# The PEER layer in one block: choosing the gathered tiles' experts during the scores, with three early fetch slots in unwritten rows

## What is computed

```python
def _peer(x, w_q, sub_keys, u_table, v_table):       # x: 512 tokens of 1024
    q = (xb @ w_q).reshape(t, PEER_HEADS, 2, PEER_HALF)          # 8 heads, 2 sides, 128
    s = jnp.einsum('thpd,hpkd->thpk', q, sub_keys)               # 128 keys a side
    top_s, top_i = lax.top_k(s, K)                               # K = 16
    cand_s = top_s[:, :, 0, :, None] + top_s[:, :, 1, None, :]
    cand_i = top_i[:, :, 0, :, None] * PEER_N_KEYS + top_i[:, :, 1, None, :]
    best_s, best_pos = lax.top_k(cand_s.reshape(t, PEER_HEADS, K * K), K)
    idx = jnp.take_along_axis(cand_i..., best_pos, axis=-1)      # 16 of 16384 experts a head
    gate = jax.nn.softmax(best_s, axis=-1)
    h = jax.nn.gelu(jnp.einsum('thkd,td->thk', u_table[idx], xb))
    return jnp.einsum('thk,thkd->td', gate * h, v_table[idx])
...
x = _layer_norm(DN_ALPHA * x + _peer(x, ...), ln2_g, ln2_b)
```

## Time and profile before

| | |
|---|---|
| median of 3 runs | 2939.73 us (2935.13 to 2944.8) |
| profiled execution, time | 2941.49 us |
| its span, first to last instruction | 2938.8 us |
| mean granted TensorE clock | 0.917 |
| busy: PE, DVE, ACT, POOL | 85%, 66%, 36%, 23% of the span |
| DMA moved | 646.82 MB, mean 220 GB/s |
| block peer starts | about 1784 us |
| hidden rows end, products end | about 2303, 2746 us |
| last dot, last add | about 2489, 2927 us |

### The profile page before, as it was taken

One profiled execution on the slowest core, in us unless ns is written; L12 is line 12 of the kernel. 1 busy time (PEld: TensorE's weight loads), 2 busy tenths in 40 slices (PEclk: granted clock), 3 DMA queues, 4 the chain that ended last, 5 costly groups with the idle time before them and its releaser, 6 DMA issues. The chain is left out here.

```text
span 2938.8 us, 32174 instructions
## 1 busy us (share of the span) xinstructions
PE 2486.3 (85%) x11638; PEld 1856.6 (63%) x11638; DVE 1944.8 (66%) x3302; ACT 1058.6 (36%) x1868; POOL 668.4 (23%) x626
## 2 busy tenths in 40 slices
PE   4988759999969998768889898999999999999300
PEld 2875547888856865567777687889988644444100
DVE  5648448888853245755536478976878555666998
ACT  3248437788843246411013331117776000000000
POOL 0000012112210000200000001334544444644674
PEclk7999859999989999889889999999999999999755
DMA  7850255887742312200012224778999999999997
GB/s 272 261 200 31 58 229 219 318 310 271 296 175 62 95 53 56 81 22 1 1 40 91 76 74 175 262 277 298 362 345 338 367 383 396 410 409 409 410 408 263
DMA packets 254877, 646.82 MB, mean 220 GB/s; under 512 B 25216, under 2 KB 123776, under 8 KB 239232
## 3 DMA queue, kind: packets, MB, share of 16 engines
q1 hardware_dynamic: 172640, 367.89, 34.9%
q0 software_dynamic: 82080, 276.88, 24.9%
HBM read 654.11 MB, written 34.60 MB: 234 GB/s over the span
## 5 line engine op out<-in xcount | busy, mean ns | idle before, releaser
L2664 POOL DMA_INDIRECT sp_rows<-in_u_rows,sp_flat x256 | 292.6, 1143 | 992.8 <-DVE sp_flat L3010 615.3
L2673 DVE SCALAR_TENSOR_TENSOR sp_rows<-sp_rows,sp_x 128x1024 f32<-128x1024 f32 x256 | 313.8, 1227 | 160.9 <-DMA sp_rows<-in_u_rows,sp_flat 158.6
L284 DVE TENSOR_TENSOR wide_low<-wide_raw,wide_high 128x2048 fp32r<-128x2048 f32 x138 | 312.5, 2291 | 63.3 <-ACT wide_high L277 61.2
L170 DVE TENSOR_TENSOR w_low<-raw,w_high 128x1024 fp32r<-128x1024 f32 x106 | 129.7, 1225 | 279.0 <-ACT w_high L161 278.4
L2788 PE MATMUL ps<-xT,raw 128*128 128x256 f32 x1248 | 279.7, 381 | 12.5 <-PEq L2420 12.5
L277 ACT CAST wide_high<-wide_raw 128x2048 fp32r<-128x2048 f32 x138 | 261.5, 1914 | 21.9 <-PE ps L334 15.8
L2816 PE MATMUL ps<-raw,tb_made 128*128 128x512 f32 x608 | 265.3, 592 | 0.0
L2788 PEld LDWEIGHTS ps<-xT,raw 128*128 128x128 f32 x1248 | 235.5, 191 | 43.4 <-issue 12.7
L2816 PEld LDWEIGHTS ps<-raw,tb_made 128*128 128x128 f32 x608 | 115.4, 190 | 144.9 <-issue 144.9
L2682 DVE SCALAR_TENSOR_TENSOR sp_x<-sp_rows,sp_coef,sp_x 128x1024 f32<-128x1024 f32 x128 | 162.9, 1286 | 48.7 <-DMA sp_rows<-in_v,sp_flat 43.2
L2682 DVE SCALAR_TENSOR_TENSOR sp_x<-xT,sp_coef,sp_x 128x1024 f32<-128x1024 f32 x128 | 163.6, 1286 | 45.9 <-DMA xT<-in_v,sp_flat 45.4
(11 more groups left out here) (515 smaller groups left out, 5244.7 us busy)
## 6 DMA issues: line engine op xcount, KB each, us to landing
wide_raw<-in_w_experts SPq DMA_DIRECT2D x96, 1024.0 KB
raw<-in_u SPq DMA_DIRECT2D x78, 512.0 KB
raw<-in_v SPq DMA_DIRECT2D x76, 512.0 KB
tb_ring<-in_v SPq DMA_DIRECT2D x52, 512.0 KB
tb_ring<-in_u SPq DMA_DIRECT2D x50, 512.0 KB
ada_raw<-in_ada_w SPq DMA_DIRECT2D x24, 1024.0 KB, 7.3
raw<-in_w_in SPq DMA_DIRECT2D x42, 512.0 KB, 3.8
raw<-in_attn_w_in SPq DMA_DIRECT2D x24, 512.0 KB, 4.5
```

The costliest lines, as they stand in the source:

```text
L170: self.m.nc.vector.tensor_tensor(self.m.w_low[:, n % AHEAD, :], self.m.raw[:, n % RAW, :], self.m.w_high[:, n % AHEAD, :].bitcast(F32), AL ...
L284: self.m.nc.vector.tensor_tensor(self.low_of[:, n % self.READY, :], self.raw[:, n % self.RAW, :], self.high_of[:, n % self.READY, :].bitca ...
L2664: self.m.nc.gpsimd.indirect_dma_start(out=self.ring[self.slot(g)], out_offset=None, in_=src, in_offset=bass.IndirectOffsetOnAxis(ap=self.f ...
L2673: self.m.nc.vector.scalar_tensor_tensor(out=rows, in0=rows, scalar=1.0, in1=self.x[:, tile, :], op0=ALU.mult, op1=ALU.mult, accum_out=self ...
```

## The change

peer_scores is gone; its work is the first part of peer's block, with no barrier between.

- DVE searches only tiles 2 and 3 in the scores. After chunk 9's low part (LOWS_FIRST = 10) and the searches of heads 0 to 3 it chooses tile 2's heads 0 to 3. The low parts of the later chunks are made in that choice's steps (low_step, ten of them).
- Then it searches heads 4 to 7, chooses the other half of tile 2, and tile 3; then searches (in groups of four) and chooses tile 0 and tile 1.
- choose works on a range of heads. EARLY_DOTS holds 66 dots, ROW_DOTS two or three a row. The softmax of tiles 2 and 3 comes after the last dot.
- The first 64 fetches use three slots in activation rows 48 to 59 (FIRST_AT), so ACT's row 48 waits for 64 dots. Fetch 64 waits for the other half of tile 2 and for the last weight chunk, and uses the old slots.
- FIRST_QUAD is 60 (was 56). Eight transposes of x (tile 2) come between two chunks of the queries, the other eight after the scores.

The core of the diff:

```diff
-EARLY = (2, 3, 0)
-ORDER_TILES = (2, 3, 0, 1)
-FIRST_QUAD = 56
+FIRST_QUAD = 60
+FIRST_DOTS, FIRST_AT = 64, 48
...
+        self.first = [words[:, FIRST_AT * DT + k * D:FIRST_AT * DT + (k + 1) * D] for k in range(3)]
...
     def slot(self, g):
-        return g % GATHERS if g < DOTS else (g - DOTS) % LATE_GATHERS
+        if g < FIRST_DOTS:
+            return g % len(self.first)
+        return (g - FIRST_DOTS) % GATHERS if g < DOTS else (g - DOTS) % LATE_GATHERS
...
+        if g in (0, FIRST_DOTS, SLOTS_EACH):
+            pool.wait_ge(self.flat_made, (0, FIRST_DOTS, SLOTS_EACH).index(g) + 1)
+        if g == FIRST_DOTS:
+            self.m.stream.done(pool, "peer_q", 2 * HEADS - 1)
+        if g == DOTS + GATHERS:
             pool.wait_ge(self.spare_free, 1)
...
-    early = [0] * 10 + [1] * 10 + [1] * 10 + [2] * 5 + [1] * 10
-    rows = [2 if r > FIRST_QUAD else 0 for r in range(KEYS)]
+    tops, choice = [1, 2, 2, 2], [1] * 10
+    early = tops + [1, 0] * 5 + choice + 2 * ([3] * 4 + choice)
+    rows = [2 + r % 2 if r > FIRST_QUAD else 0 for r in range(KEYS)]
...
+            for n in range(2, HH + 1):                     # PE
+                if n < HH:
+                    queries(n)
+                score(n - 1)
+                if n == X_TURNS[0] - 1:
+                    pe.wait_ge(shifted, KT)
+                    turn_x(0)
+            turn_x(1)
             for r in range(KEYS):
                 hidden(r)
...
             def row(r):                                    # ACT
                 act.wait_ge(table.used, r + 1)
+                if r == FIRST_AT:
+                    act.wait_ge(sparse.consumed, FIRST_DOTS)
...
+            def low_of(n):                                 # DVE
+                if n < HH:
+                    m.stream.done(dve, "peer_q", n)
+                    m.stream.low(dve, "peer_q", n)
+            def top_keys(h):
+                dve.wait_ge(copied, 2 * h + 2)
+                first_tops(nc, link, table, [(tt, 2 * h + side) for tt in SPARSE for side in range(2)])
...
-            for n in range(TT):
-                choose(n)
-                finish(n)
-                if n >= 1:
+            for n in range(LOWS_FIRST):
+                low_of(n)
+                if n % 2 == 1 and n >= 3:
+                    top_keys((n - 3) // 2)
+            choose(SPARSE[0], 0, HEADS // 2, low_step)
+            for h in range(HEADS // 2, HEADS):
+                top_keys(h)
+                step()
+            choose(SPARSE[0], HEADS // 2, HEADS, step)
+            choose(SPARSE[1], 0, HEADS, step)
+            for n, tt in enumerate(DENSE):
+                for a in range(0, 2 * HEADS, 4):
+                    first_tops(nc, link, table, [(tt, k) for k in range(a, a + 4)])
+                    step()
+                if n:
                     softmax(n - 1)
-            softmax(TT - 1)
+                choose(tt, 0, HEADS, step)
+            softmax(len(DENSE) - 1)
...
             dots(DOTS)
+            for n in range(len(DENSE), TT):
+                softmax(n)
...
-EXP_ROWS = (6, 16, 28, 46)
+EXP_ROWS = (36, 54, 125, 126)
+DIFFED_AT = (4, 5, 2, 3)
+LOWS_FIRST = 10
```

More of the change, by code:

```diff
@@ L2641, in slot, with rows @@
     def slot(self, g):
-        return g % GATHERS if g < DOTS else (g - DOTS) % LATE_GATHERS
+        if g < FIRST_DOTS:
+            return g % len(self.first)
+        return (g - FIRST_DOTS) % GATHERS if g < DOTS else (g - DOTS) % LATE_GATHERS
+    def rows(self, g):
+        k = self.slot(g)
+        if g < FIRST_DOTS:
+            return self.first[k]
+        return (self.ring + self.late)[k]
     def which(self, g):
@@ L2681, in add @@
             dve.wait_ge(self.consumed, g - len(SPARSE) + 1)
-        self.m.nc.vector.scalar_tensor_tensor(out=self.x[:, tile, :], in0=self.ring[self.slot(g)],
+        self.m.nc.vector.scalar_tensor_tensor(out=self.x[:, tile, :], in0=self.rows(g),
                                               scalar=self.coef[:, tile, s:s + 1], in1=self.x[:, tile, :],
@@ L2763, in _ @@
         def _(sp):
-            for k in range(RAW, 2 * KEYS):
+            sp.dma_start(keys, m.i["keys"].rearrange("p (h k) -> p h k", k=KEYS)).then_inc(keys_loaded, 16)
+            for n in range(HH):
+                m.stream.load_after(sp, "peer_q", n)
+            sp.wait_ge(m.split_done, m.stream.total)
+            for k in range(2 * KEYS):
+                if k == RAW:
+                    m.stream.done(sp, "peer_q", HH - 1)
                 table.load(sp, k)
@@ L2933, in step, with rest @@
                 dots(next(early))
-            def every(n, one):
-                for k in range(n - 1):
-                    one(k)
-                link(one(n - 1))
-            def choose(n):
-                tt = ORDER_TILES[n]
-                val, idx, idxf, cand, crest, best, pos = (table.val[:, tt], table.idx[:, tt], table.idxf, table.cand, table.crest,
-                                                          table.best, table.pos)
-                part, whole, parts, ranks, eq = table.part, table.whole, table.parts, table.ranks, table.eq
-                e4 = crest.rearrange("p h c -> p (h c)").rearrange("p (a h k) -> p a h k", a=len(STRIPS), k=K)
-                if tt not in EARLY:
-                    for h in range(0, 2 * HEADS, HEADS):
-                        first_tops(nc, link, table, [(tt, a) for a in range(h, h + HEADS)])
-                    for _ in range(5):
-                        step()
+            def rest(k):
+                dve.wait_ge(highs, k + 1)
+                nc.vector.scalar_tensor_tensor(out=low[:, k, :], in0=m.xT[:, k, :], scalar=m.v("ln1_b")[:, k:k + 1],
+                                               in1=high[:, k, :].bitcast(F32), op0=ALU.add, op1=ALU.subtract
+                                               ).then_inc(lows, 1)
@@ new lines, in _, with low_step, choose, every @@
+            later_lows = iter(range(LOWS_FIRST, HH))
+            def low_of(n):
+                if n < HH:
+                    m.stream.done(dve, "peer_q", n)
+                    m.stream.low(dve, "peer_q", n)
+            def low_step():
+                low_of(next(later_lows, HH))
+            def top_keys(h):
+                dve.wait_ge(copied, 2 * h + 2)
+                first_tops(nc, link, table, [(tt, 2 * h + side) for tt in SPARSE for side in range(2)])
+            def choose(tt, h0, h1, step):
+                hs, n = slice(h0, h1), h1 - h0
+                sides_of = slice(2 * h0, 2 * h1)
+                val, idx, idxf = table.val[:, tt, sides_of], table.idx[:, tt, sides_of], table.idxf[:, sides_of]
+                cand, crest, best, pos = (x[:, hs] for x in (table.cand, table.crest, table.best, table.pos))
+                part, parts, ranks = (x[:, :, hs] for x in (table.part, table.parts, table.ranks))
+                whole, eq, gates = table.whole[:, hs], table.eq[:, hs], gates_of(tt)[:, hs]
+                e4 = table.crest.rearrange("p h c -> p (h c)").rearrange("p (a h k) -> p a h k", a=len(STRIPS), k=K)[:, :, hs]
+                def every(one):
+                    for a in range(n - 1):
+                        one(a)
+                    link(one(n - 1))
```

154 lines of the change are left out of this document (115 added, 39 removed).

## The result

The changed kernel takes 2968.6 us (median of four runs, 2967.5 to 2973.9), the kernel before 2937.4 in the same comparison (2930.3 to 2944.8): ratio 1.011, interval 1.0081 to 1.0138, some 31 us slower. The forecast was 2930 with a range of 2903 to 2960, and 0.30 for slower. The profiled execution took 2973.9 us, its span is 2971.2.

The account below looks back on a forecast made before the run. From 1988 on, work was taken as a stock of DMA units draining near DMA's best rate. Gate rows from 2051, hidden rows to 2367, products to 2810, then adds and norms gave 2930 us, range 2903 to 2960.

Parts of the forecast that it names:

- Part 1: Scores' end: first fetch issues at 1777, 34 us earlier; PE's hidden rows start at about 1773, not 1784.4.
- Part 2: DVE's choosing from 1777: searches, choices, 66 dots and 13 us of fetch waits, ending at 2025.
- rival B: Choosing: the three-slot ring starves it in every burst; waits of 40 us, 2957, slower; chance 0.20.
- Part 3: Halt at row 48 on 64 dots: PE stands some 60 us, released at 2013.5; gate rows start at 2051.
- Part 5: After the hidden rows: products end at 2810, then the last adds and norms; span 2927.
- part 4: Gate rows at 2.5 dots: DMA moves 0.725 units/us, 4.8 us a row; hidden rows take 316 us, to 2367.
- rival C: Gate rows bound by fetch latency, a slot's round not shortening: 161 dots × 2.17 = 350 us; 2964, slower; chance 0.10.
- A: Gate rows: the ring of four feeds PE fully, rows stay at 4.35 us; 24 us less, 2906; chance 0.20.
- D: Gate rows: DMA held at the 361 GB/s seen there, 332 us; 2946; chance 0.08.

Follow-up runs that it names:

- b5r2: The kernel before with five slots for u rows, nine for v rows and four table slots, still two dots a row: 2915.8 us, ratio 0.9932.
- a2e39: The changed kernel with four slots, 2 dots a row, 39 early dots instead of 66, and row 48 waiting for 32 dots: 2939.1 us, ratio 1.0005.
- a2: The changed kernel with two dots a gate row as before, instead of two or three: 2949.7 us, ratio 1.0069.
- a5: The changed kernel with a fifth fetch slot, taken from the table ring (four table slots instead of five): 2922.4 us, ratio 0.9978.
- a5h32: a5 with 32 instead of 64 fetches in the activation rows, so ACT's row 48 waits for 32 dots: ratio 0.9911.
- a5e39: The changed kernel with five slots, 2.5 dots a row, 39 early dots instead of 66, and row 48 waiting for 32: 2904.6 us, ratio 0.9913.
- b5: The kernel before with five slots for u rows, nine for v rows, four table slots, and 2.5 dots a gate row: 2901.2 us, ratio 0.9875.
- a4t4: Control: the changed kernel with four table slots instead of five, still four slots for u rows: 2971.8 us, ratio 1.0138.
- ahalf: The changed kernel with each dot from the 65th on covering 512 of 1024 columns, fetches whole: 2941.8 us (one run).

## Why the prediction was wrong

**Where it was right.** Part 1: fetch and hidden rows 3 and 1.5 us later than forecast, with the 2.7 us of upstream delay in both. Part 2: choosing ended at 2024.1 against 2025, but by two errors that cancel, a start 3 us later and 8.1 us of waits for fetches instead of 13; the three-slot ring starved nothing, so rival B falls. Part 3: PE's release at 2013.2 (2013.5 forecast), gate rows from 2049.9 (2051); PE went on until 1967 and stood 46.5 us, not some 60, which changes nothing, since only the release counts. Part 5: from the end of the hidden rows to the end of the span 557.5 us against 560. The window of the halt shows the clock:

```profile
1957.00:2013.00 56.00, 9.72 (x46) 8.20 (x44) 52.98 (x222) 0.68 (x3) 17.53 (x17) 0.63 0.58 197
```

PE is busy for 9.7 of 56 us, at a granted clock of 0.63, so mostly at 1.2 GHz; its first 20 matmuls after the halt take 5.98 us, where 16 take 3.62 later (the timeline above), a loss of about 1.5 us against the 2 forecast. The Trainium skill (TensorE: Matmul & The Clock Gate, "The HAM clock gate") has an idle TensorE at 1.2 GHz and a busy one at 2.4; the trace agrees.

**The step that failed: part 4's rate.** It took "four slots reached 12 dots in 27 us plus a slice per 3.45 = 0.73 units/us", and the same from 81 dots in 186 us, and held the sum fixed, so that slower slices would leave room for quicker dots. Both rows say something else: 27 / 12 = 2.25 us a dot and 186 / 81 = 2.30, times four slots 9.0 and 9.2 us a round. In both stages DVE was either busy (17.5 and 101.1 us) or waiting for a fetch, over the whole window:

```profile
DVE sp_rows L2673 <- DMA sp_rows<-in_u_rows,sp_flat: 9.5, 9, 3.8
...
DVE sp_rows L2673 <- DMA sp_rows<-in_u_rows,sp_flat: 84.7, 78, 3.0
```

The first line is of 2276 to 2303, the second of 2303 to 2489. The dots were at the ring's limit in both, and slices only filled what was left; that a fifth slot brought the same dots to 2.08 us (b5r2) bears it out. Slower slices could free nothing for them. In the changed kernel a dot in these rows takes 5.50 / 2.5 = 2.20 us, and the hidden rows last 364 us instead of 316. Those 48 us, less 1 in the start and 2.5 in part 5, are the 44 by which the span missed (2971.2 against 2927). Part 4's bounds were PE's own pace (292) and a rate of DMA (332); neither knew the ring, so neither could hold 364. The second was also read from one window: 361 GB/s is 2050 to 2100, and over all of before's gate rows it is 342, which is 0.65 units/us and would have given 351 us.

**It was rival C.** It had the mechanism and the place, and its 350 us were short for one reason: it used 2.17 us a dot, half of the 4.35 us of one full window in the earlier trace rows. Before's gate rows take 4.50 on average (1991.5 to 2274.9), so 2.25 a dot, and 161 × 2.25 = 362. It got 0.10, and the prediction gives no reason against it. The waits for fetches in those rows were the sign that the ring was near its end: 48.9 us of waits in 283 us, on 52 of some 123 dots, and 0.3 us with a fifth slot.

**A** falls (5.50 us a row, not 4.35). **D** is not what held it: 361 GB/s was no limit, since five slots drew 372 and the products 409. The Trainium skill's limit of about 358 GB/s on the HBM side (DMA: Bandwidth & Descriptors, "Where 436 GB/s comes from") is exceeded in both; one core runs here, and the section itself points to a measurement of 425 GB/s. That GpSimd's slower issues could matter (part 2) did not show in the 8.1 us of waits. Part 2's "the row agrees" says too much: in before, from 1811 to 1893, the six issues that start beside a 2048-wide TENSOR_TENSOR, compare or multiply, take 2.74 or 2.75 us and the four beside a 2048-wide TENSOR_REDUCE 0.94, but no row shows that the first is in a two-port mode.

**What the whole change is worth, by parts.** From ratios times 2937: a2e39 +1, a2 +20, changed +32. So the one block, the earlier fetch, the moved searches and 39 early dots come to nothing; 27 further early dots with the halt on 64 cost 19; 2.5 dots a row cost 12, each known to about 8 us. With five slots the first two can be told apart: the halt on 64 costs 20 (a5 against a5h32) and the 27 dots nothing (a5h32 against a5e39). With four slots that split was not run. Why the single block brings no gain although it starts the gathered work 31 us earlier was not taken apart further; the searches of tile 0, now behind the scores, are the likely counterweight. The lowest times are b5's (2901.2) and a5e39's (2904.6), against befores of 2937.1 and 2931.3; b5 has the lower ratio. Once the ring has five slots, the change's other parts add nothing to the kernel before.

**Left open**: why a fetch needs about 7 us from issue to landing. That four table slots changed nothing (a4t4), and that the round grows to 9.6 with a fifth slot while GB/s rises, fits fetches that queue behind each other in engines at a share of 0.92 to 0.97; no run separated a queue from a fixed latency. Nor is it shown what holds the rows at 0.71 to 0.73 units/us with five slots, where the products with nine reach 409 GB/s, 0.78.

## What to carry to other kernels

Two streams that share the DMA engines need not be one stock of units. Work out for each ring its round (slots × time per use), compare it across stages, and where it is the same at different loads while the consumer shows waits, the ring is the first suspect: if it sets the pace, more uses per row lengthen the row, whatever GB/s is left. First make sure that no other engine gives the same pace, as PE nearly did here at two dots a row. Here one slot more was worth more than the whole reordering, and an edit that cost 19 us with four slots paid 17 with five. Don't count on the round to stay: it grew from 8.8 to 9.6 us, and the gain was smaller than slots over round had promised.

## What the runs showed that was not expected

- One 512 KB slot more raised the rate in the same rows from 330 to 373 GB/s, at a DMA share of 0.93 against 0.97: a share of 0.93 was no sign that the transfers were at their limit.
- Halving DVE's dots gave back a third of their time: 78 us less work, 46 us more waiting, rows 27 us shorter in all (ahalf).
- Starting the gate rows 40 us later, with 27 more dots done, left the time as it was (a5h32 and a5e39, 0.9911 and 0.9913), while the 16 us later start with the halt on 64 dots, with no dot gained, cost 20 (a5).
